# A hybrid decoder step on one core: sample keys among the projections, output matrices and gelu on ScalarE and GpSimd, last state outputs behind index scores, first picks taken from slots

## The reference

```python
u, q, k, v, qi, ki, wi = jnp.split(h @ w_in, SPLITS, axis=-1)
# state-space heads: h_t = Lbar h_{t-1} + Bbar u_t, then Re(C h) + D u
y = jax.nn.gelu(y.reshape(B, L, D_SSM))
y = y * jax.nn.sigmoid(y @ w_glu)
# index scores choose the keys of each query
s = einsum('bqh,bqhs->bqs', w, relu(einsum('bqhd,bsd->bqhs', qi, ki) * IDX_DIM ** -0.5))
_, idx = lax.top_k(s, topk)
# second layer: top 2 of 8 experts per row
top_v, top_i = lax.top_k(t @ router_w, 2)
out = out + dense_gate[:, e:e+1] * swiglu(t, w_gate[e], w_up[e], w_down[e])   # for each e
```

## Time and profile before

| | us |
|---|---|
| median of 3 executions | 1668.84 |
| lowest, highest | 1667.83, 1671.74 |
| the profiled execution | 1667.89 |
| its span in the profile | 1666.0 |
| PE busy | 1581.0 (95%) |
| DVE busy | 1268.0 (76%) |
| ACT busy | 963.8 (58%) |
| POOL busy | 97.7 (6%) |

### The profile page before, as it was taken

One profiled execution on the slowest core, in us unless ns is written; L12 is line 12 of the kernel. 1 busy time (PEld: TensorE's weight loads), 2 busy tenths in 40 slices (PEclk: granted clock), 3 DMA queues, 4 the chain that ended last, 5 costly groups with the idle time before them and its releaser, 6 DMA issues.

```text
span 1666.0 us, 23528 instructions
## 1 busy us (share of the span) xinstructions
PE 1581.0 (95%) x7853; PEld 1275.8 (77%) x7853; DVE 1268.0 (76%) x1675; ACT 963.8 (58%) x1222; POOL 97.7 (6%) x147
## 2 busy tenths in 40 slices
PE   6998888989999669999999999999999999999998
PEld 5654454679999567888888888888888888888887
DVE  8988830155544558888988988988998998998986
ACT  2121242144443127777777777777777777777774
POOL 1385300000000000000000000000000000000000
PEclk9997888999999778999999999999999999999999
DMA  6320223435545407998998998998998998999992
GB/s 226 145 76 1 63 73 102 151 113 176 179 132 173 154 26 277 358 370 312 343 376 309 359 365 308 355 370 307 351 376 309 348 372 311 351 364 323 351 357 91
DMA packets 212887, 420.79 MB, mean 253 GB/s; under 512 B 10234, under 2 KB 56470, under 8 KB 212573
## 3 DMA queue, kind: packets, MB, share of 16 engines
q1 hardware_dynamic: 211542, 414.37, 69.4%
q10 hardware_dynamic: 622, 3.45, 0.5%
q0 software_dynamic: 672, 2.32, 0.4%
HBM read 417.50 MB, written 3.07 MB: 252 GB/s over the span
## 4 chain that ended last, share of the span: by engine, by line
PE 84%; DVE 5%; ACT 1%; issue 1%; DMA 1%; SPq 0%; POOL 0%; DVEq 0%; ACTq 0%; POOLq 0%
PE bank L1231 19%; PE bank L1236 19%; PE bank L1235 19%; PE bank L1112 3%; PE bank L1109 3%; PE bank L1113 3%; PE bank L1186 3%; PE bank L1092 2%; PE bank L1256 1%; PE bank L1194 1%; PE bank L1124 1%; PE bank L1128 1%; PE bank L1127 1%; PE bank L1029 1%; PE bank L802 1%
## 5 line engine op out<-in xcount | busy, mean ns | idle before, releaser
L2111 DVE TENSOR_TENSOR split<-raw_w,split 128x1024 fp32r<-128x1024 f32 x672 | 783.2, 1220 | 50.8 <-ACT split L1586 48.6
L1586 ACT ACTIVATE split<-raw_w 128x1024 fp32r<-128x1024 f32 x672 | 684.3, 1060 | 109.4 <-PE bank L1231 108.4
L1231 PE MATMUL bank<-split,xgr 128*128 128x512 f32 x896 | 359.3, 401 | 3.7 <-DVE split L2111 3.7
L1236 PE MATMUL bank<-split,xgr 128*128 128x512 f32 x896 | 354.6, 396 | 0.0
L1235 PE MATMUL bank<-split,xgr 128*128 128x512 f32 x896 | 354.4, 396 | 0.0
L1231 PEld LDWEIGHTS bank<-split,xgr 128*128 128x128 f32 x896 | 169.4, 189 | 41.9 <-DVE split L2111 4.5
L1236 PEld LDWEIGHTS bank<-split,xgr 128*128 128x128 f32 x896 | 169.2, 189 | 39.8
L1235 PEld LDWEIGHTS bank<-split,xgr 128*128 128x128 f32 x896 | 169.4, 189 | 37.6
L1231 PE MATMUL bank<-split,hbr 128*128 128x512 f32 x448 | 177.9, 397 | 0.0
L1236 PE MATMUL bank<-split,hbr 128*128 128x512 f32 x448 | 176.9, 395 | 0.0
L1235 PE MATMUL bank<-split,hbr 128*128 128x512 f32 x448 | 176.9, 395 | 0.0
(11 more groups left out here) (386 smaller groups left out, 1940.4 us busy)
## 6 DMA issues: line engine op xcount, KB each, us to landing
raw_w<-in_moe_gate SPq DMA_DIRECT2D x112, 1024.0 KB, 5.6
raw_w<-in_moe_up SPq DMA_DIRECT2D x112, 1024.0 KB, 6.7
raw_w<-in_moe_down SPq DMA_DIRECT2D x112, 1024.0 KB, 5.4
...
```

What stands on the lines that cost most here:

```text
L1231: first = mm(out, hi, place[:, s, 0, cols], start=start, stop=False)
L1236: last = mm(out, hi, place[:, s, 1, cols], start=False, stop=stop)
L1586: A(place[:, s, 0, :], raw_w[:, at:at + BLOCK], ACT.Copy).then_inc(sem("high_ready"), 1)
L2111: TT(place[:, s, 1, :], raw_w[:, at:at + BLOCK], place[:, s, 0, :].bitcast(F32), ALU.subtract).then_inc(sem("low_ready"), 1)
```

## The change

Six things, in the order of the program:

1. The output matrices go from DVE to ACT and POOL. ACT makes `csn3` and, per tile, four products with a factor per partition as its scale (16 x 4), between the first norm and the copies of u. POOL does the two subtractions and signals `out_mats`. The scratch `wcf` lies in the space of v now, so ACT's first key copy waits for `out_mats`.
2. The groups of the state loop are new: the 8 sample keys stand singly in the groups of the projections, from q1 on; the q rotation comes before tile 6 and the q scaling before tile 9; k projections follow around them; `y` 0, `ks`, `y` 1 have groups of their own.
3. `y` 3 stands behind the second row block of the index scores.
4. The gelu is shared out: ACT squares and makes the factor 1 + 0.044715 y^2, POOL multiplies by y, ACT makes the tanh, POOL multiplies and adds (twice the gelu, so that ACT's gate tanh takes 0.25 for 0.5 and the gate 0.25 and 0.25), ACT makes the gate, POOL applies it. DVE waits for `ssm_out` only after masking row block 0.
5. v 1 is made before the gate product.
6. In the router DVE takes slots and the first picks before the gates and tables; `slot_v` itself gets the copy of the low rows. POOL zeroes `pickTr` and `ybr`.

```diff
     dots = [("dot", t, h) for t in range(TC) for h in range(H)]
-    return dots[:H] + [("y", 3)] + dots[H:]
+    return dots[:2 * H] + [("y", 3)] + dots[2 * H:]
...
-    groups = [[], four("qis") + ["kis", "wiT"], [("q", 0)], [("q", 1), "wbd"], [("q", 2)], [("q", 3), "qn"],
-              [("k", 0)], [("k", 1)], [("k", 2)], [("k", 3), "kn"], four("qs") + keys(0, 1), keys(2, 3, 4),
-              four("qe") + keys(5), keys(6, 7) + four("ks"), ["kidT", ("y", 0), ("y", 1)], four("ke") + [("y", 2)]]
+    groups = [[], four("qis") + ["kis", "wiT"], [("q", 0), "wbd"], [("q", 1)] + keys(0), [("q", 2)] + keys(1),
+              [("q", 3), "qn"] + keys(2), four("qs") + keys(3), [("k", 0)] + keys(4), [("k", 1)], four("qe") + keys(5),
+              [("k", 2)] + keys(6), [("k", 3), "kn"] + keys(7), ["kidT", ("y", 0)], four("ks"), [("y", 1)],
+              four("ke") + [("y", 2)]]
...
-    f += [("v", 0)] + [("glu", c) for c in range(4)] + [("v", 1)]
+    f += [("v", 0), ("v", 1)] + [("glu", c) for c in range(4)]
...
-        wcf = [rtmp[:, 4 * T + k * 512:4 * T + (k + 1) * 512].rearrange("p (j s) -> p j s", j=NJ) for k in range(2)]
+        wcf = [zv[:, k * 512:(k + 1) * 512].rearrange("p (j s) -> p j s", j=NJ) for k in range(2)]
...
+            nc.gpsimd.memset(quarter, 0.25)
...
+            pool.wait_ge(sem("out_products"), 1)
+            for r in range(2):
+                last = TT(cf4[:, :, r, :], cf4[:, :, r, :], wcf[r], ALU.subtract)
+            last.then_inc(sem("out_mats"), 1)
+            pool.wait_ge(sem("out_mats"), 1)
...
+            pool.wait_ge(sem("gelu_factor"), 1)
+            TT(ga, gb, yv, ALU.mult).then_inc(sem("gelu_arg"), 1)
+            pool.wait_ge(sem("gelu_tanh"), 1)
+            pool.wait_ge(sem("gelu_arg"), 1)
+            link(TT(gb, gb, yv, ALU.mult))
+            TT(yv, gb, yv, ALU.add).then_inc(sem("gelu"), 1)
+            pool.wait_ge(sem("gelu"), 1)
+            pool.wait_ge(sem("glu_gate"), 1)
+            TT(yv, ga, yv, ALU.mult).then_inc(sem("ssm_out"), 1)
+            pool.wait_ge(sem("ssm_out"), 1)
...
+            for i in range(2):
+                emptied(pool, ("xn", 2, i))
+            nc.gpsimd.memset(pickTr[:, :].bitcast(F32), 0.0)
+            nc.gpsimd.memset(ybr[:, :].bitcast(F32), 0.0).then_inc(sem("late_zeros"), 1)
...
             value_rows(0)
+            value_rows(1)
...
-            value_rows(1)
...
+            act.wait_ge(sem("factors"), 1)
+            act.wait_ge(sem("mats_in"), 16)
+            A(csn3, c_m[:, :, 1, :], ACT.Copy, scale=-1.0).then_inc(sem("csn_ready"), 1)
+            act.wait_ge(sem("csn_ready"), 1)
+            for j in range(NJ):
+                re, im = fr_[:, j:j + 1], fi_[:, j:j + 1]
+                A(cf4[:, j, 0, :], c_m[:, j, 0, :], ACT.Identity, scale=re)
+                A(wcf[0][:, j, :], c_m[:, j, 1, :], ACT.Identity, scale=im)
+                A(cf4[:, j, 1, :], csn3[:, j, :], ACT.Identity, scale=re)
+                last = A(wcf[1][:, j, :], c_m[:, j, 0, :], ACT.Identity, scale=im)
+            last.then_inc(sem("out_products"), 1)
...
+                    if b == 0:
+                        act.wait_ge(sem("out_mats"), 1)
...
+            emptied(act, ("y", 3))
+            act.wait_ge(sem("last_state"), 1)
+            A(ga, yv, ACT.Square).then_inc(sem("gelu_square"), 1)
+            act.wait_ge(sem("gelu_square"), 1)
+            A(gb, ga, ACT.Identity, scale=0.044715, bias=ones[:, 0:1]).then_inc(sem("gelu_factor"), 1)
+            copy_rows(("v", 0), z3["v"])
             act.wait_ge(sem("gelu_arg"), 1)
             A(gb, ga, ACT.Tanh, scale=GELU_C).then_inc(sem("gelu_tanh"), 1)
-            copy_rows(("v", 0), z3["v"])
+            copy_rows(("v", 1), z3["v"])
             for c in range(4):
                 filled(act, ("glu", c))
-                A(ga[:, c * T:(c + 1) * T], ps(("glu", c))[:, 0:T], ACT.Tanh, scale=0.5).then_inc(free(("glu", c)), 1)
-
-            copy_rows(("v", 1), z3["v"])
+                A(gb[:, c * T:(c + 1) * T], ps(("glu", c))[:, 0:T], ACT.Tanh, scale=0.25).then_inc(free(("glu", c)), 1)
+            emptied(act, ("glu", 3))
+            A(ga, gb, ACT.Identity, scale=0.25, bias=quarter).then_inc(sem("glu_gate"), 1)
 
             def exps(t, h0, h1):
...
-            def out_matrices():
-
-                dve.wait_ge(sem("mats_in"), 16)
-                w1, w2 = wcf
-                TT(w1, c_m[:, :, 0, :], wide(fr_, 32), ALU.mult)
-                link(TT(w2, c_m[:, :, 1, :], wide(fi_, 32), ALU.mult))
-                link(TT(cf4[:, :, 0, :], w1, w2, ALU.subtract))
-                TT(w1, c_m[:, :, 0, :], wide(fi_, 32), ALU.mult)
-                link(TT(w2, c_m[:, :, 1, :], wide(fr_, 32), ALU.mult))
-                STT(cf4[:, :, 1, :], w1, -1.0, w2, ALU.mult, ALU.subtract)
-                TS(csn3, c_m[:, :, 1, :], -1.0, None, ALU.mult).then_inc(sem("out_mats"), 1)
-                dve.wait_ge(sem("out_mats"), 1)
-
...
-                    if name[1] == MATS_AT:
-                        out_matrices()
...
-            emptied(dve, ("y", 3))
-            dve.wait_ge(sem("last_state"), 1)
-            yv = uT.rearrange("p c t -> p (c t)")
-            link(TT(ga, yv, yv, ALU.mult))
-            link(TS(ga, ga, 0.044715, 1.0, ALU.mult, ALU.add))
-            TT(ga, ga, yv, ALU.mult).then_inc(sem("gelu_arg"), 1)
...
-                if r == GELU_AT:
-                    dve.wait_ge(sem("gelu_tanh"), 1)
-                    link(STT(gb, gb, 1.0, yv, ALU.add, ALU.mult))
-                    TS(yv, gb, 0.5, None, ALU.mult).then_inc(sem("gelu"), 1)
-                    dve.wait_ge(sem("gelu"), 1)
...
-            for c in range(4):
-                emptied(dve, ("glu", c))
-            link(TS(ga, ga, 0.5, 0.5, ALU.mult, ALU.add))
-            TT(yv, ga, yv, ALU.mult).then_inc(sem("ssm_out"), 1)
-            dve.wait_ge(sem("ssm_out"), 1)
...
             mask_logits(0)
+            dve.wait_ge(sem("ssm_out"), 1)
             mask_logits(1)
...
+            filled(dve, "rank")
+            rp = ps("rank")[:, 0:4 * NE].rearrange("p (t e) -> p t e", t=4)
+            link(TT(slot_v, sel, rp[:, 0:TC, :], ALU.mult))
+            link(TS(slot_v, slot_v, -1.0, None, ALU.add))
+            link(nc.vector.tensor_copy(slot_v[LOW_ROWS:LOW_ROWS + 24, 2, :], slot_v[0:24, 2, :]))
+            for t in range(TC):
+                last = TS(pick[:, t, :], iota, slot_v[:, t, 0:1], None, ALU.is_equal)
+            last.then_inc(sem("pick_ready"), 1)
             dve.wait_ge(sem("router_exp"), 1)
             link(TS(g12[:, 2, :], g12[:, 1, :], 1.0, None, ALU.add))
...
-            filled(dve, "rank")
-            rp = ps("rank")[:, 0:4 * NE].rearrange("p (t e) -> p t e", t=4)
-            link(TT(slot_v, sel, rp[:, 0:TC, :], ALU.mult))
-            link(TS(slot_v, slot_v, -1.0, None, ALU.add))
...
-            link(nc.vector.tensor_copy(pslot[LOW_ROWS:LOW_ROWS + 24, 0:PASSES, 2], pslot[0:24, 0:PASSES, 2]))
...
-            for t in range(TC):
-                last = TS(pick[:, t, :], iota, pslot[:, 0, t:t + 1], None, ALU.is_equal)
-            last.then_inc(sem("pick_ready"), 1)
-            for i in range(2):
-                emptied(dve, ("xn", 2, i))
-            nc.vector.memset(pickTr[:, :].bitcast(F32), 0.0)
-            nc.vector.memset(ybr[:, :].bitcast(F32), 0.0).then_inc(sem("late_zeros"), 1)
```

5 lines of the change are left out of this document (3 added, 2 removed).

## The result

The changed kernel takes 1650.45 us (median of 4, 1647.58 to 1652.8), the kernel before 1668.34 beside it (1667.44 to 1671.74): a ratio of 0.9891, 95% interval 0.987 to 0.9912, or 18.2 us less (14.7 to 21.7). Forecast were 1652, range 1644 to 1661. The total came out, but in part by luck: the loop lost 5.3 us where nothing was forecast, and the gelu's stage and the stretch behind it gained 3.6 more than forecast.

What follows compares the result with a forecast made beforehand. In the state loop PE and DVE were both taken to be near their limit, PE leading during projections, DVE after. 1667.89 + 1.3 - 3.4 - 5.4 - 9.3 = 1651.1, median 0.95 above: 1652 us, range 1644 to 1661.

Steps and rivals of the forecast that it cites:

- Start: Before the state loop: ACT's products hidden, POOL's subtractions take turns with DVE; tile 0 starts 1.3 us later (0 to 2.9).
- The loop: State loop: DVE's saved 7.49 us worth nothing; tile 15 at 161.5 against 160.25, 1.3 us lost, start included.
- Tile 15 after 165: State loop: one of the signs the prediction named beforehand as showing it wrong; its upper bound for tile 15 was 165.
- the walk: Prediction's step-by-step timing; in the state loop tile 8 ends at 115.7, tile 11 at 131.7, tile 15 at 159.0 at full rate.
- The second rival: State loop: PE at half rate from first key to k3, seven projections and keys doubled, 34 us, so 1686; chance 0.04.
- Index scores: Index-score stretch: y3's move lets eight dots fill DVE's idle 5.24 us; 25.7 shrinks to 22.3, 3.4 us gained (2 to 5).
- Gelu: Index scores to second mask: DVE freed, v1 before the glu; gain 6.9 (glu at full rate) or 3.8 us, 5.4 taken.
- a mean, 5.4: Gelu stage: gain taken between 6.9 us with the glu at full rate and 3.8 with it partly at half rate.
- The third rival: No half-rate stretch in the state loop (tile 15 at 157.5) and the glu at full rate: 1646 us; chance 0.10.
- The first rival: Pick rounds: POOL's products hold them up, a loss of 1.7 us instead of a gain of 5.4; 1659 us; chance 0.10.
- Router: Router: early picks let the gather follow the transposes at full rate; first expert matmul at 621.9, 9.3 us gained.
- The fourth rival: Router gives less: half-rate gather, or the loop's entry costs more; 1655 us; chance 0.06.

Runs made afterwards that it cites:

- e2: The kernel before with only the output matrices moved to ACT and POOL, groups in the old order: 1669.34 us, ratio 1.0003.
- e7: The changed kernel with the q and k norm sums each moved behind the next pair of state inputs: 1642.98 us, ratio 0.9856.
- e6: The changed kernel with y3 back behind the first row block's dots: 1655.66 us, ratio 0.9922.
- e4: The kernel before with only the gelu shared out to ACT and POOL and v1 ahead of the glu: 1659.12 us, ratio 0.9943.
- e10: The changed kernel with the two late zeroings (pickTr, ybr) back on DVE behind the pass tables: 1652.11 us, ratio 0.9908.
- e3: The kernel before with the whole loop part, output matrices on ACT and POOL and the new order of groups: 1675.44 us, ratio 1.004.

## Why the prediction was right, and where it was not

**Start: right.** 1.3 forecast, 0.9 measured. ACT's 64 products took 0.30 each as estimated, but started 0.21 apart, so they were done at 31.5 and not at 37. The subtractions did take turns with DVE (0.68 to 1.78), which gave up 2.2 us and not 2.9.

**The loop: wrong in size.** The step said tile 15 at 161.5, bounds 157.5 to 165; it was at 166.4, and the five profiles with this order lie from 165.3 to 167.3. "Tile 15 after 165" was one of the prediction's own signs of being wrong, and it came. Its first half held: DVE's 7.5 us are worth nothing (e2), idle before tile 5 was 5.13 (4.7 forecast), tile 8 ended at 116.6 (115.7); a wait of 1.93 before tile 4, which the walk didn't have, was made up in part by a q rotation beside tile 5 shorter by 1.0. The term that failed is "I expect PE to fall to half rate once ... 2.5 us, about half of the matmuls that follow". Behind q0 it fell three times: from 78.0 to 81.4 on q2 (1.7 lost, in the wait before tile 4), from 112.2 to 122.4 on scaling, key, pair and k2, and from 153.1 to 163.4 on the k scaling and y2, whose skip waited 3.10. Tile 11 was 3.7 behind the walk (135.35 for 131.7): 1.0 from tile 9's pair, which started at 116.67 for 115.7, 1.0 from that pair (2.13 for 1.13) and 1.7 from k2 (5.64 for 4.0, to the next key). From tile 11 to tile 15 it took 31.1, the walk had 27.3 and the one stretch's 2.5. The second rival (projections lose their clock) had the mechanism and a wrong size: two of seven projections, not all, so 3.4 us on them and not 34. The 5 us of idle time before tiles 5 and 11, which the prediction had right, were the norms' placing: 3 us of each went in e7, and 3.4 at tile 15.

**Index scores: right in sum, by two errors that cancel.** 3.4 forecast, 2.9 between the two kernels, 4.3 by e6. The eight dots were to fill the idle time of 5.24, and 2.48 of it stayed, with PE at half rate from 170.2 to 180.4. Against that, about six dots were to stretch beside POOL, by 2.0 in all. They did not: those of the second row block took 1.11 for two and 2.78 for five, 0.56 each, where seven took 3.69 before, 0.53 each, which is 0.2 in all.

**Gelu: right in its case, undervalued in sum.** The prediction counts from 185.97, half a microsecond behind E; on E's count its second mask is at E+29.3 (full rate) or E+32.4. It was E+29.1, and E+28.8 in e4. The step failed only where it took a mean, 5.4: idle time of 1.58 in front of the glu left the clock at 1.00. The third rival had this half, too, but its gain in the loop didn't come. The 2.5 us of idle it forecast were 0.9 too long; POOL's products took 2.56 each and not 3.13. It also kept the shift as it was from there on; to the router's first transpose another 1.9 was gained. In e4, 7.7 at the mask became 7.4 there, so that 1.9 is not a gain of the gelu's part as such. The first rival (POOL holds up the rounds) fell: a round kept its 2.17.

**Router: right**, 9.3 forecast and 9.3 found, 9.6 alone; picks at 603.3 and the gather's 4.66 instead of 4.42. Counted from the first transpose, which is 5.7 earlier, the walk's end of DVE's tables (617.2) is 611.5, and there it was. POOL's zeroing took 2.2 us and not 3.5. The fourth rival (a half-rate gather) fell. Its side remark on the loop entry (that table load, high and low part follow) is what hides the zeroing in e10.

**Sum.** By medians the parts are -11.8 (router), -9.5 (gelu), +6.7 (loop), and -5.2 for y3 by e6: -19.8, against -18.2 measured, and each of them has an interval of some 2 to 3 us to either side. By these medians the forecast gave 4.1 too little to the gelu, 2.5 to the router and 1.8 to y3, and the loop cost 5.4 more than it said (in e3's profile 1.7 of that lies behind E, in v2). That these misses nearly cancel is luck; the forecast of 1652 is right to 1.5 us, its terms only to 1.8 to 5.4.
